# Strassen-style pairs for the last output columns, with the forget panel and four gate columns moved

## The reference, cut to what matters

```python
y = g[:, :, 0] * ua + g[:, :, 1] * ub + g[:, :, 2] * uc
return x + y @ w_out
```

## Time and profile before

| what | value |
|---|---|
| median of 3 runs | 2167.94 us (2161.6 to 2169.49) |
| the profiled execution, its time | 2160.38 us |
| the profiled execution, its span | 2158.8 us |
| PE busy | 99% of the span |
| PE weight load busy | 84% |
| DVE busy | 71% |
| ACT busy | 41% |
| POOL busy | 3% |
| HBM traffic | 140 GB/s over the span |

### The profile page before, as it was taken

How to read it: one execution, slowest core, us unless ns; L and a number is a source line. 1 busy time by engine, 2 the same in 40 slices (tenths; PEclk the granted TensorE clock), 3 DMA queues, 4 the chain that set the end, 5 groups by cost and what they waited for, 6 DMA issues and landing times.

```text
span 2158.8 us, 34650 instructions
## 1 busy us (share of the span) xinstructions
PE 2127.1 (99%) x11664; PEld 1822.1 (84%) x11664; DVE 1539.2 (71%) x2580; ACT 893.5 (41%) x1573; POOL 61.6 (3%) x117
## 2 busy tenths in 40 slices
PE   7999999999999999999999999999999999999999
PEld 6788888888888999999997888888787887888887
DVE  7888877785658888888867666666777776665333
ACT  6433454433335444444443444444545444222221
POOL 0000000000000000000000000000000000000000
PEclk9999999999999999999999999999999999999999
DMA  9766423674444433433432222222222223554443
GB/s 381 276 228 247 169 92 98 230 269 141 145 146 132 147 133 113 144 133 114 142 105 95 91 87 88 92 88 83 69 88 69 89 88 120 168 169 152 143 145 111
DMA packets 83684, 303.26 MB, mean 140 GB/s; under 512 B 9317, under 2 KB 11765, under 8 KB 75265
## 3 DMA queue, kind: packets, MB, share of 16 engines
q1 hardware_dynamic: 71568, 258.24, 35.7%
q0 software_dynamic: 9280, 39.33, 5.3%
q10 hardware_dynamic: 2738, 4.47, 0.5%
HBM read 280.74 MB, written 21.27 MB: 140 GB/s over the span
## 4 chain that ended last, share of the span: by engine, by line
PE 80%; DVE 6%; ACT 4%; DMA 3%; issue 3%; DVEq 3%; ACTq 1%; POOL 0%; SPq 0%; POOLq 0%
PE bank L422 19%; PE bank L423 19%; PE bank L424 19%; PE bank L1163 6%; PE bank L1165 6%; PE bank L1164 6%; DMA w_raw<-stream 3%; DVE w_lo L416 3%; ACT w_hi L406 1%; PE bank L545 1%; PE bank L576 1%; DVEq L411 1%; PE bank L558 1%; ACT probs L626 1%; PE bank L1047 0%
## 5 line engine op out<-in xcount | busy, mean ns | idle before, releaser
L422 PE MATMUL bank<-x_hi,w_hi 128*128 128x512 f32 x2224 | 876.9, 394 | 5.2 <-DVEq L680 1.9
L424 PE MATMUL bank<-x_hi,w_lo 128*128 128x512 f32 x2224 | 866.7, 390 | 0.0
L423 PE MATMUL bank<-x_lo,w_hi 128*128 128x512 f32 x2224 | 866.4, 390 | 0.0
L416 DVE TENSOR_TENSOR w_lo<-w_raw,w_hi 128x512 fp32r<-128x512 f32 x524 | 362.9, 692 | 443.7 <-ACT w_hi L406 420.2
L406 ACT ACTIVATE w_hi<-w_raw 128x512 fp32r<-128x512 f32 x524 | 331.3, 632 | 690.1 <-PE bank L424 562.0
L422 PEld LDWEIGHTS bank<-x_hi,w_hi 128*128 128x128 f32 x2224 | 417.8, 188 | 103.2 <-issue 7.8
L424 PEld LDWEIGHTS bank<-x_hi,w_lo 128*128 128x128 f32 x2224 | 417.8, 188 | 88.1
L423 PEld LDWEIGHTS bank<-x_lo,w_hi 128*128 128x128 f32 x2224 | 418.2, 188 | 84.3 <-issue 0.2
L1163 PE MATMUL bank<-x_hi,pw_hi 128*128 128x256 f32 x1176 | 333.1, 283 | 0.9 <-DVE pw_lo L1936 0.8
L1164 PE MATMUL bank<-x_lo,pw_hi 128*128 128x256 f32 x1176 | 332.8, 283 | 0.0
L1165 PE MATMUL bank<-x_hi,pw_lo 128*128 128x256 f32 x1176 | 332.8, 283 | 0.0
(11 more groups left out here) (200 smaller groups left out, 1761.1 us busy)
## 6 DMA issues: line engine op xcount, KB each, us to landing
w_raw<-stream SPq DMA_DIRECT2D x262, 512.0 KB, 3.8
pw_raw<-stream SPq DMA_DIRECT2D x84, 512.0 KB, 4.6
wmod<-w_mod_rows SPq DMA_DIRECT2D x32, 1024.0 KB, 6.6
front_raw<-stream SPq DMA_DIRECT2D x16, 1024.0 KB, 9.8
wmod<-w_mod_rows POOLq DMA_DIRECT2D x16, 1024.0 KB, 5.7
sig_store<-logits POOLq DMA_DIRECT2D x45, 256.0 KB, 2.6
sig_back<-sig_store SPq DMA_DIRECT2D x8, 768.0 KB, 5.5
gate_sig<-sig_store SPq DMA_DIRECT2D x7, 768.0 KB, 5.9
```

The lines of the kernel that those rows point to most:

```text
L416: nc.vector.tensor_tensor(w_lo[:, q, :], raw_quarter(s), w_hi[:, q, :].bitcast(F32), ALU.subtract).then_inc(lo_ready, 1)
L422: nc.tensor.matmul(bank_ap[:, :tokens], hi, x_hi[:, kx, :], start=start, stop=False)
L423: nc.tensor.matmul(bank_ap[:, :tokens], hi, x_lo[:, kx, :], start=False, stop=False)
L424: return nc.tensor.matmul(bank_ap[:, :tokens], lo, x_hi[:, kx, :], start=False, stop=stop)
```

## The change

The first two output panels of out stay. The other 14 become seven pairs that go through the same seven products as the gate pairs, with sums over halves of the tokens of y (`sums_of_y`, made in every second branch panel, the last set ahead of the first out panel) and their high and low parts made during the two plain out panels. `product` of the first two factors may start before the last low part of these sums; the third waits for all (`t_ready`). `back_and`, `first_result` and `second_result` put the results together. The tile of x that is added back is scaled beforehand: in each of 14 branch panels POOL loads a tile from `x_store` into one buffer `x_prime`, DVE scales it (`x_primed`), POOL stores it again, waits for the store to land, and loads the next.

The forget panel goes ahead of the three gates_1 panels (4 panels and 16 steps now); its result is worked on in these steps, with the last two sums after the products 4 and 7 of the first pairs. The windows b lose that work, and POOL stores `c_store` early.

Of the 16 gate columns 12 stay in gate_b (two in even panels, one in odd ones, at step 2); the last four go to panels 4, 6, 8 and 10 of pool_out, into two buffers of their own.

The diff, cut to its core:

```diff
-          ("group_b", 2), ("gate_b", KT // 2), ("pool_out", KT), ("gates_1", 3), ("forget", 1),
+          ("group_b", 2), ("gate_b", KT // 2), ("pool_out", KT), ("forget", 1), ("gates_1", 3),
           ("b", 4 * HEADS_B // 2), ("a", 2 * (2 + 2 * GROUPS)), ("c", 2 * HEADS_C),
-          ("gated", 4), ("branch", KT - 1), ("out", KT)]
+          ("gated", 4), ("branch", KT - 1), ("out", 2)]
...
+OUT_PAIRS = (KT - 2) // 2
...
+        x_prime = sb("x_prime", [P, T], F32, at_scratch + 6 * KB)
+        x_back = sb("x_back", [P, 2, T], F32, at_upper + 2 * KB)
+        result = sb("result", [P, 2, T], F32, at_scratch + 2 * KB)
...
+        f_a = sb("f_a", [P, T], F32, at_scratch + 4 * KB)
+        f_b = sb("f_b", [P, T], F32, at_scratch + 6 * KB)
+        f_c = sb("f_c", [P, T], F32, at_scratch + 2 * KB)
...
+            def back_load(n):
+                if n < 2:
+                    sp.wait_ge(y_ready, KT)
...
-                    back_loads(At(slot, 2, i), slot)
+                    sp.wait_ge(result_ready, n - 1)
+                sp.dma_start(x_back[:, n % 2, :], x_store[n, :, :]).then_inc(x_back_loaded[n % 2], 16)
+            first = 4 * PAIRS
+            for n in range(2):
+                load_panel(sp, At(FIRST["out"] + n))
+            for n in range(2):
+                back_load(n)
+            for l in range(6):
+                load_factor(first + l)
+            sp.wait_ge(xp_stored, 16 * (KT - 2))
+            for p in range(OUT_PAIRS):
+                back_load(2 + 2 * p)
+                for l in range(4 * p + 6, min(4 * p + 8, 4 * OUT_PAIRS)):
+                    load_factor(first + l)
+                back_load(3 + 2 * p)
+                for l in range(4 * p + 8, min(4 * p + 10, 4 * OUT_PAIRS)):
+                    load_factor(first + l)
...
+            panel(pe, At(FIRST["forget"]), At(RESULT["forget"]), x1_hi, x1_lo, {3: x1_sums}, ready=hn_ready)
...
-            panel(pe, At(g), At(r), x1_hi, x1_lo, {3: x1_sums}, ready=hn_ready)
-            panel(pe, At(g + 1), At(r + 1), x1_hi, x1_lo)
-            panel(pe, At(g + 2), At(r + 2), x1_hi, x1_lo)
+            for b in range(3):
+                panel(pe, At(g + b), At(r + b), x1_hi, x1_lo)
             lower, upper = slice(0, HALF), slice(HALF, T)
...
             panel(pe, At(g + 1), At(r + 1), x1_hi, x1_lo)
-            with steps(pe, 1, KT // 2) as i:
-                for n in range(2):
-                    panel(pe, At(g + n, 2, i), At(r + n, 2, i), x1_hi, x1_lo)
+            for l in range(PRODUCTS, PRODUCTS + 7 * OUT_PAIRS):
+                if l == PRODUCTS + 2:
+                    pe.wait_ge(t_ready, KT)
+                product(Factor(l))
...
+                    act.wait_ge(w_used, 4 * g + 4)
+                    nc.scalar.activation(f_c[:, :], acc[r % 2][:, :], ACT.Copy).then_inc(f_raw_ready, 1)
+                    act.drain().then_inc(acc_free[r % 2], 1)
...
+                if s == 7:
+                    act.wait_ge(f_abs, 1)
+                    nc.scalar.activation(f_c[:, :], f_b[:, :], ACT.Exp, scale=-1.0)
+                    act.drain()
+                    nc.scalar.activation(f_c[:, :], f_c[:, :], ACT.Ln, bias=1.0).then_inc(f_ln, 1)
...
+            def last_sigmoid():
+                sigmoid_of(At(2 * PAIRS + 2), 1)
+                act.preload_act_table_set("natural_log_exp_and_others")
+                nc.scalar.activation(blocks_r[:, :], blocks[:, :], ACT.Copy)
+                nc.scalar.activation(ones_r[:, :], ones[:, :], ACT.Copy).then_inc(sums_of_ones_ready, 1)
+            windows(act, act_window, last_sigmoid)
...
+            for s in range(8):
+                split_hi(act, At(4 * g + s))
+                token_sums_hi(KT // 2 + s)
+                if s == 6:
+                    act.wait_ge(lo_ready, 4 * PANELS)
+                    factor_hi(Factor(PRODUCTS))
+                if s == 7:
+                    act.wait_ge(w_used, 4 * PANELS - 2)
+                    factor_hi(Factor(PRODUCTS + 1))
+                    store_result(0)
+            act.wait_ge(w_used, 4 * PANELS)
+            for l in range(PRODUCTS, PRODUCTS + 7 * OUT_PAIRS):
+                act_product(l)
+            store_result(KT - 1)
...
                     split_lo(dve, At(4 * (FIRST["gate_b"] + i) + s))
-                    if s in (1, 3):
-                        mod_column(2 * KT + 2 * i + s // 2)
-                    if s == 3:
-                        mod_biases(2 * KT + 2 * i, 2, 0.0)
...
                         yg_low(KT - 1)
+                    if m in (4, 6, 8, 10) and s == 1:
...
+                    token_sums_lo(s - 3)
...
+                    dve.wait_ge(f_raw_ready, 1)
+                    nc.vector.tensor_tensor(f_a[:, :], f_c[:, :], r_both[:, :], ALU.mult)
+                    dve.drain()
+                    nc.vector.tensor_scalar(f_a[:, :], f_a[:, :], col("b_forget"), None, ALU.add)
+                    dve.drain()
+                    nc.vector.scalar_tensor_tensor(f_b[:, :], f_a[:, :], -1.0, f_a[:, :], ALU.mult, ALU.max).then_inc(f_abs, 1)
+                if s == 8:
+                    dve.wait_ge(f_ln, 1)
+                    nc.vector.tensor_scalar(f_a[:, :], f_a[:, :], 0.0, None, ALU.min)
+                    dve.drain()
+                    nc.vector.tensor_tensor(f_b[:, :], f_c[:, :], f_a[:, :], ALU.subtract)
+                    dve.drain()
+                if s == 9:
                     plain_gate(0)
-                    token_sums_lo(2)
-                if 6 <= s < 10:
-                    token_sums_lo(s - 3)
-                if s == 10:
...
                     plain_gate(1)
                     factor_lo(Factor(0))
-                if s == 11:
+                if s == 15:
...
+                    forget_sum(dve, 7 + l // 7)
             with steps(dve, 1, PAIRS // 3 - 1) as i:
                 for l in range(21):
                     dve_product(l, i)
...
+            def x_primed(n):
+                dve.wait_ge(xp_loaded, (n - 1).times(16).value())
+                nc.vector.scalar_tensor_tensor(x_prime[:, :], x_prime[:, :], col("final_g", n), r_one[:, :],
+                                               ALU.mult, ALU.mult).then_inc(xp_made, 1)
+            def sums_of_y(k):
+                two = tile(x3, k.times(2) + 1)
+                one = tile(x3, k.times(2))
+                dve.drain()
+                nc.vector.tensor_tensor(one[:, HALF:], one[:, HALF:], one[:, :HALF], ALU.subtract)
+                dve.drain()
+                nc.vector.tensor_tensor(two[:, HALF:], two[:, HALF:], one[:, HALF:], ALU.subtract)
+                dve.drain()
+                nc.vector.tensor_tensor(two[:, :HALF], two[:, :HALF], two[:, HALF:], ALU.subtract)
+                nc.vector.tensor_tensor(one[:, :HALF], two[:, HALF:], one[:, :HALF], ALU.subtract)
+                dve.drain().then_inc(t_made, 1)
...
                     split_lo(dve, (n + (FIRST["branch"] - 1)).times(4) + s)
                     if s == 0:
                         branch(n - 1, 2, *before)
+                    if s == 1 and k is not None:
+                        sums_of_y(k)
                     if s >= 2:
                         branch(n, s - 2, slot, loaded)
+                    if s == 2 and n.lowest() > 1:
+                        x_primed(n)
                     if s == 3:
                         low_part(n - 1, x1_hi, x1_lo, y_hi, y_split)
             branch_beat(At(1), 1, At(1), (0, None))
             with steps(dve, 0, KT // 2 - 1) as i:
...
+            def back_and(n, terms_so_far):
+                dve.drain()
+                dve.wait_ge(x_back_loaded[n % 2], 16 * (n // 2 + 1))
+                dve.wait_ge(result_stored[n % 2], 16 * (n // 2) + ONE)
+                nc.vector.tensor_tensor(result[:, n % 2, :].rearrange("p (a t) -> p a t", a=2), terms_so_far,
+                                        x_back[:, n % 2, :].rearrange("p (a t) -> p a t", a=2), ALU.add)
+                dve.drain()
+            def first_result(pair):
+                n = 2 + 2 * (pair.c - PAIRS)
+                back_and(n, pair_sum[:, :].rearrange("p (a t) -> p a t", a=2))
+                dve.wait_ge(product_done, 7 * pair.c + 5)
+                nc.vector.tensor_tensor(result[:, n % 2, :], result[:, n % 2, :], row_1[:, :], ALU.add).then_inc(row_read, 1)
+                dve.drain().then_inc(result_ready, 1)
+            def second_result(pair, j):
+                n = 3 + 2 * (pair.c - PAIRS)
+                back_and(n, later_terms[:, :].unsqueeze(1).broadcast_to([P, 2, HALF]))
+                dve.wait_ge(product_done, 7 * pair.c + 7)
+                nc.vector.tensor_tensor(result[:, n % 2, :], result[:, n % 2, :], row_2[j][:, :], ALU.add).then_inc(row_read, 1)
+                dve.drain().then_inc(result_ready, 1)
+            g = FIRST["out"]
+            sums_of_y(At(KT // 2 - 1))
+            for s in range(8):
+                split_lo(dve, At(4 * g + s))
+                if 0 < s < 7:
+                    token_sums_lo(KT // 2 + s - 1)
```

(27 more changed lines are left out.)

277 lines of the change are left out of this document (111 added, 166 removed).

## The result

The changed kernel takes 2147.53 us (median of 4 runs, 2146.27 to 2147.93), the kernel before 2164.77 beside it (4 runs, 2161.12 to 2169.49); the ratio is 0.9922, 95% interval 0.9906 to 0.9938. It is faster by 17 us. The profiled execution took 2147.93; the prediction's own figure for the like of its profile was 2149.4.

What follows compares the result with a forecast made beforehand. PE, busy 99%, was taken to bound the kernel. The terms -11.2 + 0.2 + 0.4 - 1.3 - 1.1 + 1.5 + 0.5 summed to -11.0, taking the median 2167.94 to 2157 us; range 2150 to 2164.

Steps and rivals of the forecast that it cites:

- Output pairs: Output stage: a pair costs PE 20.16 us against 21.76 for two panels, so seven pairs save 11.2 us.
- +0.2 for their start: Start of the output pairs: DVE's preparation just fits the two plain out panels, costing 0.2 us, from below 0 to above 2.
- Sums of y: Branch panels: DVE's sums almost exactly fit, delaying PE's bank slightly in seven panels; +0.4 us, from 0 to 3.
- x' loop: Branch panels: POOL's store and load take about 10 us, hidden in a panel of 10.88 by under 1; cost 0.
- Gate columns: End of gate_b: moving a column off DVE lets `gated(15)` start sooner and removes PE's stall; -1.3 us, from 0 to -1.3.
- Out of the windows: Windows b: without the forget work PE's wait for q_t goes; -1.1 us, from 0 to -1.1.
- Into gates_1: Panels of gates_1: added forget work makes DVE late, PE 1.1 and 0.9 late, 0.5 gone; +1.5 us, from -0.5 to +4.
- In the first pairs: First gate pairs: `forget_sum(8)` comes while DVE catches up; +0.5 us, from 0 to 1.
- rival A: Start of pairs, branch bank and gates_1: new stalls eat 4 to 9 us, or removed stalls stay; 2160 to 2166, chance 0.26.
- B: Branch panels: POOL's loop exceeds 10.88 us and clocks 14 panels, making the kernel slower; 2177, chance 0.08.
- C: Gates_1 and the branch panels do not stall at all, so more gain: -14.1 us, 2154, chance 0.19.
- D: Gates_1: stalls falling together lower PE's clock, adding one piece of 1.3 to 1.7 us; 2159; chance 0.47 together with the forecast.

Runs made afterwards that it cites:

- e2: The kernel before with only the output pairs, sums of y and x' loop; forget panel and gate columns where they were: 2157.56 us, ratio 0.9973.
- e1: The changed kernel with all edits, run again beside the kernel before: 2148.68 us, ratio 0.9931 to the kernel before.
- e10: The changed kernel as it is, run again as the measure for two reordered versions: 2147.68 us, ratio 0.9925 to the kernel before.
- e7: The changed kernel with each tile of x in the branch stage loaded twice in sequence, making POOL's loop longer: 2175.47 us in one run.
- e5: The kernel before with only the sixteenth gate column moved into pool_out on DVE, all loads left in place: 2159.38 us, ratio 0.9983.
- e8: The kernel before with the last fourteen of sixteen gate row tiles loaded by halves, columns left on DVE: 2159.36 us, ratio 0.9983.
- e3: The kernel before with only the last four gate columns and their loads moved beside the pooled output: 2160.27 us, ratio 0.9986.
- e13: The kernel before, unchanged, profiled a second time: 2165.35 us.
- e14: The kernel before, unchanged, profiled a third time: 2162.48 us.
- e11: The changed kernel with DVE's third branch gate in the gated stage moved ahead of the last four low parts: 2146.70 us, ratio 0.9919 to the kernel before.
- e12: The changed kernel with the gated-stage gate moved as in e11, plus two DVE moves in gates_1: 2146.94 us, ratio 0.9920 to the kernel before.

## Why the prediction was wrong, step by step

- **Output pairs, -11.2 with +0.2 for their start.** Nearly right. Fourteen panels of 10.88 are 152.3; the seven pairs run from 2000.62 to 0.12 behind 2142.72, 142.2: -10.1. The difference to -11.0 is mostly the start, where PE is 0.84 late between starts at the third product, the one named, for a factor's low part that ended at 2007.32. The 0.120 per matmul held. By the figure of the Trainium skill for an isolated matmul (TensorE: Matmul & The Clock Gate, Back-to-back issue gap) the pairs would have saved an estimated 16.7; this stream of weight loads and matmuls ran at 227 and 120 ns, and 10.1 is measured.
- **Sums of y, +0.4.** The bounds held in all but e2, and the 0.4 was too small: the fifteen branch panels took 1.3 more than 15 x 10.88 in the changed kernel's profile, 0.6 in e1, 2.1 in e10 and 3.4 in e2. The mechanism is the one named: PE loses about 0.1 at the twelfth tile of every second panel, and 0.43 (1.31 in e10) at the start of one.
- **x' loop, 0.** Right: DVE waited 1.4 in two times, and the rival's mechanism is real once the loop is longer (e7). The loads took 4.5 and not the 2.6 of the stores. The Trainium skill's formula (DMA: Bandwidth & Descriptors, Anatomy of one DMA) gives an estimate of 2.6 for both, so a plan by it would have seen over twice the margin. The prediction says that the first row agrees with the formula; it is the second, with 2.6.
- **Gate columns, "-1.3 (from 0 to -1.3)".** This is the step that failed. The wait went, as said, but its size was wrong, and its cause was only half of it: late raw weights were left out. In the three profiles of the kernel before, the sums of x1 start 1.7 to 6.8 us later than in e10, and in those of the whole without the edit 7.7 to 11.9. By the means the edit is worth 4.1 alone (0.6 to 5.4 by the ratio) and about 9 in the whole. The column's 2.29 on DVE adds to the wait but isn't needed for it, late raw weights are: e5 has a wait of 3.54 without the column, e8 has none with it.
- **"The median of the runs shown is 2167.94, 7.6 above it; from there 11.0 less is 2157".** The same step once more, and a second miss in the base. It took the 7.6 for scatter that both kernels share. Some 4 of it (the kernel before has means of 2162.9 to 2164.6 over 81 runs, its profiled execution 2160.38) is largely what this wait costs in ordinary executions, and the edit removes it: e1 and e10 scatter by 3 to 4 us, the kernel before by 14. The other 3 or 4 is the draw of three runs: the median of the four beside the changed kernel was 2164.77. So of the 9.5 between 2157 and 2147.5, 3.2 is the base and 6.2 the change. One view that I didn't read would have pointed at the wait: ACT waits in gate_b, 46.2 us in 15 times.
- **Forget work.** Out of the windows -1.1: right, the wait for `q_t` is gone. Into gates_1 +1.5: 1.19 and 0.57 from start to start, which is 0.96 and 0.34 late, at the two places named (1.1 and 0.9 forecast), while 0.5 went. In the first pairs +0.5: wrong in sign. The first three pairs took 1.2 more than 3 x 20.16 before and 0.3 here (1.5 in e1, 0.1 in e10), and 2.0 to 2.6 more in e3, e5, e8, e13 and e14, whose profiles all have the wait for `pw_lo` at 1.3 to 2.0. So "PE still does not wait" over the pairs, and rival A's "21 gate pairs ran without such stalls", did not hold even before: the first pairs stalled, and least of all in the profile that the prediction read. Since e2, with the forget panel where it was, doesn't stall there either, what removes these waits is not shown.
- **The rivals.** A fell: new waits came (0.96, 0.34, 0.43 and 0.84, 2.6 in sum), but the removed ones went. B is shown to be possible and not reached. C was nearest in time, for another reason. D: in the first profile of before the half clock followed the gated stage's wait, in the profile of after it did not, which is 1.6 of the 12.4.
- **The range.** Its lower end was to be C less the 6 of scatter. That is 2148, not the 2150 written.

In averages of the profiles, the sums start at 667.05 in the three of before and 663.18 in after, e1 and e10: 3.9, with 1.3 forecast. The rest is 1495.1 over the six that leave it as it was (before, e3, e5, e8, e13, e14) and 1483.4 over those three: 11.7, with 9.7 forecast. Together they are 15.6, near the 16.0 of the means.

With the gate columns at their measured 4 to 9 us in place of 1.3, the same sum from the median gives about 2149 to 2154 with the 2167.94 of the three runs first shown, and 2146 to 2151 with the 2164.77 of the four that stand beside the changed kernel.

## What to carry to other kernels

When the runs of a kernel scatter by more than the change is worth, the profile is one draw: ask what in it could be worse in the others, and whether the edit removes just that. Read the waits of the engines that feed the bound engine, too: here a feeder waited for a transfer fifteen times in ninety microseconds, and the bound engine lost 1 us to it in one execution and 5 in the next. Where DVE was nearly full, a wait moved by order came back later (e11, e12).
